# High parts of two k-tiles first, then their low parts, in part of a two-block float32 kernel

## The reference, cut to what matters

```python
proj = z @ w_in[l]                       # 2048 -> 3072
h = h + y @ w_out[l]                     # out projection
q = (zc @ peer_wq)                       # then top 16 of 16384 experts for each of 8 heads
act = gelu(einsum('chkd,cd->chk', u, zc)); ... einsum('chk,chkd->cd', w, v)
...
proj = einsum('bsd,de->bse', h, w_in[l]) + b_in[l]      # 2048 -> 9216
merged = sigmoid(gate_sb) * o_sb + sigmoid(gate_cv) * o_cv
y = einsum('bsd,de->bse', merged, w_o[l])
f = square(relu(einsum('bsd,df->bsf', h, w_up[l])))
f = einsum('bsf,fd->bsd', f, w_down[l])
```

## Time and profile before

| | |
|---|---|
| median of 3 runs | 3244.68 us (3234.92 to 3253.92) |
| the profiled execution | 3256.32 us |
| its span, first to last instruction | 3254.4 us |
| mean granted TensorE clock | 0.991 |
| TensorE matmul busy | 3178.3 us, 98% |
| VectorE busy | 2180.6 us, 67% |
| ScalarE busy | 1692.5 us, 52% |
| GpSimd busy | 675.0 us, 21% |
| transfers | 615.35 MB, mean 189 GB/s |

### The profile page before, as it was taken

One profiled execution on the slowest core, in us unless ns is written; L12 is line 12 of the kernel. 1 busy time (PEld: TensorE's weight loads), 2 busy tenths in 40 slices (PEclk: granted clock), 3 DMA queues, 4 the chain that ended last, 5 costly groups with the idle time before them and its releaser, 6 DMA issues.

```text
span 3254.4 us, 46963 instructions
## 1 busy us (share of the span) xinstructions
PE 3178.3 (98%) x18222; PEld 2773.0 (85%) x18222; DVE 2180.6 (67%) x3000; ACT 1692.5 (52%) x2629; POOL 675.0 (21%) x690
## 2 busy tenths in 40 slices
PE   8999989999999999999999999999998999999998
PEld 7788878888888888888888888888887888888887
DVE  7857999864655555555646569999675855555564
ACT  6554357644545444454545655566656444444444
POOL 1423420321312222131313420000242100000003
PEclk9999999999999999999999999999999999999999
DMA  6465547766565656565566555555665555665664
GB/s 240 150 200 178 179 151 230 238 189 203 187 213 186 211 187 213 187 208 189 187 213 188 185 185 163 173 174 175 189 191 170 164 190 190 189 191 190 189 192 138
DMA packets 177854, 615.35 MB, mean 189 GB/s; under 512 B 18273, under 2 KB 35041, under 8 KB 176225
## 3 DMA queue, kind: packets, MB, share of 16 engines
q1 hardware_dynamic: 157824, 572.59, 55.5%
q10 hardware_dynamic: 19808, 39.76, 3.5%
HBM read 593.41 MB, written 18.87 MB: 188 GB/s over the span
## 4 chain that ended last, share of the span: by engine, by line
PE 81%; DVE 12%; issue 3%; ACT 2%; POOL 1%; DMA 1%; ACTq 0%; DVEq 0%; POOLq 0%
PE G L412 53%; PE G L413 27%; DVE lo L1025 5%; DVE CV L1333 2%; DVE oneB L1308 1%; DVE tS L1085 1%; ACT hi L647 1%; PE M L500 1%; DVE tS L1031 0%; DVE oneA L1310 0%; ACT oneB L824 0%; POOL X L1543 0%; DVE XC L1072 0%; POOL acc L1548 0%; PE M L481 0%
## 5 line engine op out<-in xcount | busy, mean ns | idle before, releaser
L412 PE MATMUL G<-ZA,hi 128*128 128x512 f32 x5120 | 1814.7, 399 | 23.4 <-DVE lo L1025 10.7
L1025 DVE TENSOR_TENSOR lo<-raw,hi 128x1024 fp32r<-128x1024 f32 x1088 | 1399.6, 1308 | 294.7 <-ACT hi L647 294.3
L413 PE MATMUL G<-ZA,lo 128*128 128x256 f32 x5120 | 1435.1, 280 | 0.0
L412 PE MATMUL G<-ZB,hi 128*128 128x512 f32 x3568 | 1253.1, 397 | 4.1 <-DVE ZB L1321 4.0
L412 PEld LDWEIGHTS G<-ZA,hi 128*128 128x128 f32 x5120 | 966.3, 189 | 253.2 <-issue 17.4
L647 ACT ACTIVATE hi<-raw 128x1024 fp32r<-128x1024 f32 x1088 | 1113.5, 1051 | 65.8 <-DMA raw<-in_pv 39.3
L413 PE MATMUL G<-ZB,lo 128*128 128x256 f32 x3584 | 1002.9, 280 | 0.0
L413 PEld LDWEIGHTS G<-ZA,lo 128*128 128x128 f32 x5120 | 970.8, 190 | 0.5
L412 PEld LDWEIGHTS G<-ZB,hi 128*128 128x128 f32 x3568 | 670.3, 188 | 166.7 <-DVE lo L1025 2.6
L654 ACT ACTIVATE tA<-G 128x256 f32<-128x256 f32 x559 | 212.2, 380 | 971.5 <-PE G L413 970.9
L413 PEld LDWEIGHTS G<-ZB,lo 128*128 128x128 f32 x3584 | 676.5, 189 | 0.0
(11 more groups left out here) (271 smaller groups left out, 1368.5 us busy)
## 6 DMA issues: line engine op xcount, KB each, us to landing
raw<-in_pu SPq DMA_DIRECT2D x256, 512.0 KB, 3.6
raw<-in_pv SPq DMA_DIRECT2D x256, 512.0 KB, 4.1
raw<-in_w_in SPq DMA_DIRECT2D x192, 512.0 KB, 3.6
raw<-in_w_up SPq DMA_DIRECT2D x128, 512.0 KB, 3.5
raw<-in_w_down SPq DMA_DIRECT2D x128, 512.0 KB, 3.5
raw<-in_w_out SPq DMA_DIRECT2D x32, 512.0 KB, 3.5
raw<-in_wq SPq DMA_DIRECT2D x32, 512.0 KB, 3.5
g_scratch<-stage ACTq DMA_DIRECT2D x16, 1024.0 KB, 4.8
```

Of the source, the lines that this page charges most:

```text
L412: pe.matmul(G[:, 0:512], hi[h % NW][:, k % 8, :], Z[:, k, :], start=first, stop=False, skip_group_check=True)
L413: m = pe.matmul(G[:, 0:256], lo[h % NRAW][:, k % 8, :], Z[:, k, 0:256], start=False, stop=last, skip_group_check=True)
L1025: dve.tensor_tensor(lo[r][:, :, :], raw[r][:, :].rearrange("p (k n) -> p k n", k=8), hi[w][:, :, :].bitcast(F32), ALU.subtract).then_inc(s ...
```

## The change

`product` is cut into `high` and `rest`. A new function gives for each unit how many k-tiles are taken at once: 2 in `ot`, `v`, `mg` and `yo` but for their first unit, in `u` from chunk 2 on, and in the second block's input products but for the first; 1 elsewhere. With 2, the order in a half becomes high, high, low, low. In every half outside groups the wait for `lo` moves behind the first one or two highs, and a wait for `hi` comes ahead of them.

```diff
-            def product(u, p, n, k, G, first, last):
-                h = POS[u][p]
+            def high(u, p, k, G, first):
+
+                w = hi[POS[u][p] % NW][:, k % 8, :]
                 Z = weights(u, p)[1]
                 if u == N - 1:
...
+                    pe.matmul(G[:, 0:512], w, Z[:, k, :], start=first, stop=False, skip_group_check=True)
+
+            def rest(u, p, n, k, G, last):
+
+                m = pe.matmul(G[:, 0:256], lo[POS[u][p] % NRAW][:, k % 8, :], weights(u, p)[1][:, k, 0:256], start=False,
+                              stop=last, skip_group_check=True)
                 if n == 7:
                     m.then_inc(s_mm, 1)
+
+            def product(u, p, n, k, G, first, last):
+                high(u, p, k, G, first)
+                rest(u, p, n, k, G, last)
+
+            def at_once(u):
+
+                st, i, c = STAGE[u]
+                if st in ("ot", "v", "mg", "yo"):
+                    return 2 if i else 1
+                if st == "u":
+                    return 2 if c >= 2 else 1
+                if st in ("gb", "ga", "qkv", "sg"):
+                    return 2 if u > F0 else 1
+                return 1
 
             def half(u, p):
                 apart = STAGE[u][0] == "mg"
                 b = BANK[u] + (p if apart else 0)
-                weights_ready(POS[u][p])
-                if apart or p == 0:
+                start, stop = apart or p == 0, apart or p == 1
+                if start:
                     bank_free(b)
-                for n, k in enumerate(weights(u, p)[2]):
-                    operand_ready(u, k)
-                    product(u, p, n, k, GB[b % 4], n == 0 and (apart or p == 0), n == 7 and (apart or p == 1))
+                ks = list(enumerate(weights(u, p)[2]))
+                step = at_once(u)
+                for x in range(0, 8, step):
+                    for n, k in ks[x:x + step]:
+                        operand_ready(u, k)
+                        if n == 0:
+                            pe.wait_ge(s_hi, POS[u][p] + 1)
+                        high(u, p, k, GB[b % 4], n == 0 and start)
+                    if x == 0:
+                        weights_ready(POS[u][p])
+                    for n, k in ks[x:x + step]:
+                        rest(u, p, n, k, GB[b % 4], n == 7 and stop)
```

More of the change, by code:

```diff
@@ L403, in bank_free @@
                     pe.wait_ge(s_join, b - 3)
-            def product(u, p, n, k, G, first, last):
-                h = POS[u][p]
+            def high(u, p, k, G, first):
+                w = hi[POS[u][p] % NW][:, k % 8, :]
                 Z = weights(u, p)[1]
                 if u == N - 1:
-                    pe.matmul(G[:, 0:256], hi[h % NW][:, k % 8, :], Z[:, k, 0:256], start=first, stop=False, skip_group_check=True)
-                    pe.matmul(G[:, 0:256], hi[h % NW][:, k % 8, :], Z[:, k, 256:512], start=False, stop=False, skip_group_check=True)
-                else:
-                    pe.matmul(G[:, 0:512], hi[h % NW][:, k % 8, :], Z[:, k, :], start=first, stop=False, skip_group_check=True)
-                m = pe.matmul(G[:, 0:256], lo[h % NRAW][:, k % 8, :], Z[:, k, 0:256], start=False, stop=last, skip_group_check=True)
+                    pe.matmul(G[:, 0:256], w, Z[:, k, 0:256], start=first, stop=False, skip_group_check=True)
+                    pe.matmul(G[:, 0:256], w, Z[:, k, 256:512], start=False, stop=False, skip_group_check=True)
+                else:
+                    pe.matmul(G[:, 0:512], w, Z[:, k, :], start=first, stop=False, skip_group_check=True)
+            def rest(u, p, n, k, G, last):
+                m = pe.matmul(G[:, 0:256], lo[POS[u][p] % NRAW][:, k % 8, :], weights(u, p)[1][:, k, 0:256], start=False,
+                              stop=last, skip_group_check=True)
                 if n == 7:
                     m.then_inc(s_mm, 1)
+            def product(u, p, n, k, G, first, last):
[10 more added lines that the diff above has]
+                return 1
             def half(u, p):
```

## The result

The new kernel takes 3238.29 us (median of 20 runs, 3235.83 to 3243.61), the old one, run beside it, 3251.84 us (20 runs, 3230.49 to 3260.80). The ratio is 0.9964, with a 95% interval of 0.9949 to 0.9978: 0.4% faster, clear of the noise by its interval, and less than the 0.5% that I called no change. The second number that counts is the scatter, lowest to highest run: 30 us before, 8 us after.

What follows compares the result with a forecast made beforehand. TensorE's own rate, busy for 98% of the span, was taken to bound the kernel. From the profiled 3256.3 us, 24.5 us for the rhythm and 1 us for earlier highs came off: 3231 us, range 3208 to 3266.

Steps and rivals of the forecast that it cites:

- The two rhythms: TensorE runs the same instruction order at 353.3 or about 346.5 ns a k-tile, changing only at a disturbance.
- The order inside pairs, 346.5 ns: In 5296 paired k-tiles, high-high-low-low was taken to run at the fast rhythm, 346.5 ns each.
- The 22.5 us from 730 to 1900 us: In that stretch, 3312 k-tiles leave the slow rhythm and save 6.8 ns each, 22.5 us.
- the out projection's rhythm: At 150 to 240 us, 256.5 k-tiles save 4.4 ns each, 1.1 us.
- the `v` units at 630 to 720 us: In that window, 258.5 k-tiles save 1.7 ns each, 0.4 us.
- the second block's input stage: Where attention's products break the stream, the paired input products were given a gain of 0.5 us.
- The sum: Whole kernel: 24.5 us from rhythm and 1 us from earlier highs, taken off the profiled 3256.3 us, give 3231 us.
- Weight loads left in the open: Under two successive lows in a pair, loads might not fit; they were taken to fit, at no cost.
- The wait for the high parts first, 1 us: In 1074 halves, highs start before the wait for lo: at most 2.4 us gained, 1 us taken.
- Drawn as before: Rival, chance 0.22: in the paired stages the rhythm is drawn again as before, no effect, 3244 us.
- Always slow: Rival, chance 0.18: pairs always run in the slow rhythm, 353.3 ns a k-tile, 3265 us.
- Faster than the fast rhythm: Rival, chance 0.14: pairs beat the fast rhythm through loads brought forward; 37 us at most, half of it 3212 us.

Runs made afterwards that it cites:

- kick_v: Old kernel with a small product of constants ahead of the second unit of each v stage from chunk 1 on: 3247.52 us, ratio 1.0000.
- kicks_pairs: New kernel with a small product of constants at the start of each stretch of 16 units from chunk 2 on: 3239.7 us, one run.
- orders_by_chunk: New kernel with 1, 4, 8, 3, 2, 1 k-tiles at once in expert chunks 2 to 7: 3245.91 us, one run.
- new_again: New kernel unchanged, run later on the same chip as kick_v: 3239.32 us, ratio 0.9951.
- pairs_mlp: New kernel with the MLP's units in pairs too, except the first unit of each down product: 3239.72 us, ratio 0.9959.
- few_waits: kick_once with three waits for operands in each first unit of v in place of sixteen: 3251.08 us, one run.
- kick_once: Old kernel with one small product of constants ahead of unit 106, two units behind the wait at 720 us: 3255.18 us, ratio 1.0007.
- kicks: Old kernel with twelve small products of constants, one per stretch of 16 units from chunk 2 on: 3245.04 us, one run.
- kicks_wide: Old kernel with twelve products of constants, each 256 columns wide in place of the 128 of kicks: 3250.92 us, one run.
- order_only: New kernel with the old waits, lo waited for ahead of a half's first high, pairs kept: 3239.73 us, ratio 0.9957.

## Why the prediction was right, point by point

*The two rhythms.* Right, and now shown and not only read from three windows: a kick of 0.22 us turned one into the other at eleven of the twelve places where it stood, and the MLP has been seen in both. The old kernel's runs fall into two groups about 20 us apart, and the pairs' runs stay within 8 us, which fits my reading of the scatter as a draw. That each slow run is slow for this reason isn't shown. What makes the draw is open: I named the 2.26 us wait at 720 us, and overlooked that the granted clock was 0.63 from 724 to 728 us behind it, so the return of the clock may set the rhythm as well as the wait.

*The order inside pairs, 346.5 ns.* The direction was right, the size off. It is the term that was mis-sized: the pairs take 348.3 ns, or 348.6 with the single first units of `v` among them, so 5296 x 2.1 ns = 11 us are missing from the sum. To 0.01 us the steps are what I took: 0.23 for each high, in a pair too, and 0.23 for two lows. I had worked out 347.5 ns from these steps and then rounded it to the fast rhythm because that was the nearer of the two that I knew. The better step was to keep the 347.5: it is within 1 ns of what was measured, and would have given 3236 us. Steps read to 0.01 us can't tell 346.5 from 348.3. The 0.118 was itself a reading of the first ten steps of the last unit only. Its 48th product starts at

```profile
3239.88 0.28 PE L413 MATMUL G<-ZB,lo 128*128 128x256 f32 x1
```

which makes the 37 steps behind the earlier trace rows 4.44/37 = 0.120 us each.

*The 22.5 us from 730 to 1900 us.* 15.6 us in the profiled pair. The smaller terms partly changed sign: the out projection's rhythm gave 1.2 us (I had 1.1), but the `v` units at 630 to 720 us were fast before and lost 0.4 (I had a gain of 0.4), and the second block's input stage lost 0.3 (I had a gain of 0.5).

*The sum.* The mechanism was right and the size was off by half: 25.5 us forecast against the profiled execution, 12.7 measured in the profiled pair. That my 3231 still lies within 8 us of the measured median is partly luck. I had set the gain against an execution that was above the median; against medians the change is worth 13.6 us, and I had 13.7 for it (3244.7 to 3231), from a median of three runs that was 7 us under the one of twenty. The agreement of 13.6 and 13.7 is luck too: two errors cancel in it.

*Weight loads left in the open.* Right that there is no large cost: eight lows in a row take 349.4 ns with their highs, no more than three in a row. A small one, 0.119 to 0.120 us for a low in a long row against 0.117, is there; whether it is the loads' no run shows. The 325 ns for a k-tile that I worked out from the Trainium skill (TensorE: Matmul & The Clock Gate, "Back-to-back issue gap") was never seen; 346.4 is the least that a long window here shows (kick_v).

*The wait for the high parts first, 1 us.* Nothing: 0.9999, within 0.1% either way. The cost of the added waits is nothing too, as predicted, and no wait for `hi` appeared on TensorE. The waits of the weight loads for `lo` shrank by 4.2 us, more than my bound of 2.4, and it still brought nothing.

*The rivals.* "Drawn as before" falls with kicks_pairs: the pairs didn't take turns. My ground against it, that a new pattern can't lock in, was a guess, and why pairs have one rhythm stays open. "Always slow" falls with the windows: 348.3 and not 353.3. (The point from which it decides is misreckoned: 3261 us goes with 346.5 + 5.7 = 352.2 ns, not 351.8.) But it is right in one stage, as to sign: `mg`, `yo` and, when tried, the MLP are 1.6 to 1.8 ns a k-tile slower in pairs than in a fast single order. "Faster than the fast rhythm" falls with the same windows, and with orders_by_chunk for longer rows.

*What I hadn't seen.* The wait at 174 us, and that it differs from one execution to the next. It was 0.3 us (of a weight load) in the old kernel's trace and 3.3 us in the new one's, but 1.0 us in new_again, the same kernel; no product waited there in kicks_pairs and pairs_mlp, which have pairs, and products waited 1.0 to 1.7 us in few_waits, kick_once and kick_v, which have the old order. So the 3.3 us and the lower clock behind it belong to that execution, which is also the slowest of the new kernel's twenty runs, and not to the change.

## What to carry to other kernels

Where one engine is busy without a gap, count its instructions in equal windows before looking for waits: two rates for the same code point to a rhythm of the engine, and it may explain the scatter between runs. An order with one rhythm can be worth more in the median than an order with a better and a worse one; its gain must be sized from its own rate, and it costs something wherever the other order was in its better one. Before a wait is put down to a change, look for it in a second trace of the same kernel. Before a step between two known rates is rounded to one of them, ask whether it may be a third.

## What the runs showed of the hardware that I had not expected

- The same stream of a 512-column and a 256-column product by turns goes at 346.7 or at 353.3 ns for the two, at a granted clock of 1.00 (the upper level) throughout, the slow one for over 1000 us without a change (the old kernel), the fast one for 500 and more (its MLP). The slow one repeats over three k-tiles (1.06 us), the fast one takes 1.04 us for three.
- Two 512-column products and then two 256-column ones take 348.3 ns for each k-tile, in five traces; three of each take 349.7, four 350.7 and eight 349.4, in one trace.
- Behind a product of 0.22 us in the stream the rhythm was another one in eleven of twelve places (kicks), and it was another one behind a start that slipped by 0.06 us (kick_once, few_waits); behind each product of twice the width it was the fast one (kicks_wide).
- After an idle time of 3.3 us TensorE went on at a granted clock of 0.50 (the lower level, 1.2 GHz), with 14 matmuls in 4 us in place of 25; in order_only, after 1.7 us at the same place, it went on at 1.00. By the Trainium skill (TensorE: Matmul & The Clock Gate, "What's actually happening") the clock has these two states and idleness brings the lower; the trace agrees.
